# A mixture-of-experts loop: the first 32 blocks without run-time tests, and the next block's rows transposed ahead of the down product

## The reference

```python
# top-1 of 4 groups, top-2 of 8 experts in it; tokens sorted by expert,
# each expert's tokens padded to whole blocks of MOE_BLOCK = 128 rows
rows = jnp.zeros((n_blocks * MOE_BLOCK, D), h.dtype).at[dest].set(h[s_tok])
...
def expert_block(args):
    xb, e = args
    return (jax.nn.silu(xb @ w_gate[e]) * (xb @ w_up[e])) @ w_down[e]

out = lax.map(expert_block, (rows.reshape(n_blocks, MOE_BLOCK, D), blk_expert)).reshape(-1, D)
return jnp.zeros((M, D), h.dtype).at[s_tok].add(out[dest] * s_w[:, None])
```

## Time and profile before

| what | value |
|---|---|
| median of 3 runs | 2845.91 us (2845.04 to 2850.43) |
| the profiled execution's own time | 2846.74 us |
| its span | 2845.0 us |
| mean granted TensorE clock over the span | 0.932 of full speed |
| matmuls of the expert loop, L2385 and L2395 | 450.6 and 225.0 us of PE |
| expert loop | about 2082 us to the end of the span |

### The profile page before, as it was taken

The page is one execution under the profiler, slowest core; times in us unless marked ns, Lnnn a source line. Parts: engine busy times, 40 slices in busy tenths (PEclk is TensorE's granted clock), DMA queues, the critical chain, the costliest instruction groups (busy, mean ns, idle before and its releaser), DMA issues. The chain is left out here.

```text
span 2845.0 us, 32921 instructions
## 1 busy us (share of the span) xinstructions
PE 2515.7 (88%) x12051; PEld 1571.1 (55%) x12051; DVE 784.1 (28%) x1523; ACT 493.2 (17%) x1315; POOL 485.7 (17%) x574
## 2 busy tenths in 40 slices
PE   6999998999779999869816999979779999999996
PEld 4446655888566676647514666634334444444443
DVE  2016442555355655424420000001221111111110
ACT  1101111333024444423200000001100000000000
POOL 1035121343130000100030000011102112211221
PEclk8999999999569999979958999989879999999998
DMA  4010300000220000056255000032258888888894
GB/s 130 30 59 30 127 2 0 1 1 1 63 32 1 1 1 1 13 151 172 68 148 148 30 1 1 0 128 77 107 198 312 313 310 309 318 312 303 310 318 127
DMA packets 186148, 331.25 MB, mean 116 GB/s; under 512 B 32901, under 2 KB 82318, under 8 KB 185822
## 3 DMA queue, kind: packets, MB, share of 16 engines
q1 hardware_dynamic: 160118, 293.08, 30.4%
q0 software_dynamic: 15472, 28.89, 3.6%
q10 hardware_dynamic: 10432, 7.57, 0.9%
HBM read 307.48 MB, written 51.37 MB: 126 GB/s over the span
## 5 line engine op out<-in xcount | busy, mean ns | idle before, releaser
L2385 PE MATMUL psum<-f_W,f_xT 128*128 128x512 f32 x1024 | 450.6, 598 | 17.0 <-DVE f_xT L2431 16.0
L2385 PEld LDWEIGHTS psum<-f_W,f_xT 128*128 128x128 f32 x1024 | 193.0, 191 | 255.8 <-issue 254.6
L1918 PE MATMUL psum<-hT,x_wg 128*128 128x344 f32 x768 | 227.8, 455 | 20.7 <-DMA x_wg<-w_in 20.7
L419 PE MATMUL psum<-w,hT 128*128 128x512 f32 (+3 forms) x576 | 225.5, 552 | 7.1 <-DMA w<-w_in 7.1
L2395 PE MATMUL psum<-f_W,f_aT 128*128 128x512 f32 x512 | 225.0, 592 | 1.2 <-DVE f_aT L2446 1.2
L1918 PEld LDWEIGHTS psum<-hT,x_wg 128*128 128x128 f32 x768 | 146.8, 191 | 97.5 <-DMA x_wg<-w_in 20.8
L419 PEld LDWEIGHTS psum<-w,hT 128*128 128x128 f32 (+1 forms) x576 | 103.6, 182 | 122.7 <-issue 107.6
L419 PE MATMUL psum<-hT,w 128*128 128x344 f32 x576 | 168.9, 454 | 0.0
L2395 PEld LDWEIGHTS psum<-f_W,f_aT 128*128 128x128 f32 x512 | 97.2, 190 | 123.4 <-issue 123.4
L1491 ACT ACTIVATE a_P<-psum,a_nmax 128x512 f32<-128x512 f32 (+4 forms) x256 | 123.0, 494 | 168.5 <-DVE a_nmax L1420 109.2
L2435 DVE TENSOR_TENSOR f_a<-f_sg,psum 128x512 f32<-128x512 f32 x32 | 22.0, 689 | 460.7 <-ACT f_sg L2416 460.7
(11 more groups left out here) (481 smaller groups left out, 3429.6 us busy)
## 6 DMA issues: line engine op xcount, KB each, us to landing
f_W<-w_gate SPq DMA_DIRECT2D x32, 2048.0 KB, 14.2
f_W<-w_up SPq DMA_DIRECT2D x32, 2048.0 KB, 20.3
f_W<-w_down SPq DMA_DIRECT2D x32, 2048.0 KB, 9.5
k_stage<-cache_nsa SPq DMA_DIRECT2D x128, 192.0 KB, 2.6
w<-w_in SPq DMA_DIRECT2D x6, 2048.0 KB, 7.9
x_wg<-w_in SPq DMA_DIRECT2D x8, 1024.0 KB, 13.7
x<-x_prompt SPq DMA_DIRECT2D x8, 512.0 KB, 4.4
o_x<-x_prompt SPq DMA_DIRECT2D x8, 512.0 KB, 4.3
```

Of the source, the lines that this page charges most:

```text
L419: ins = nc.tensor.matmul(PS[i % 4][0:m_rows, 0:n], lhsT, rhs, start=(k == 0), stop=(k == KD - 1))
L1918: ins = nc.tensor.matmul(PS[b + i][:, 0:n], wg[q % 3][:, k, i, c:c + P], hT[:, k, t0:t0 + n], start=(k == 0), stop=(k == KD - 1))
L2385: ins = nc.tensor.matmul(PS[bank][:, :], xT[par][:, k, :], w[par][:, k, :], start=(k == 0), stop=(k == KD - 1))
```

## The change

Three things are changed. First, `each_block` is written in two parts: a loop of 15 rounds and one step more covers the first 32 blocks without any test, and what lies behind block 32 is a second loop of eight rounds with the old tests, the whole of it behind one test n > NE. Second, PE's `transpose_rows` of block b+1 moves from `rest` into `first`, so that it stands behind the gate and up product of b and ahead of the down product of b-1. Third, the copies `copy_rows` on ACT and DVE move along: on ACT behind SiLU, on DVE behind the multiplication by up, both ahead of `copy_out`. POOL's and SP's own functions are the same as before, except that the tests around them are gone.

```diff
-            n = engine.value_load(blocks[0:1, MAXBLK:MAXBLK + 1], min_val=MINBLK, max_val=MAXBLK)
+            n = engine.value_load(blocks[0:1, MAXBLK:MAXBLK + 1], min_val=NE, max_val=MAXBLK)
             first(0, 1, 1, 0)
             rest(0, 1, 1)
-            with engine.Fori(0, MAXBLK // 2) as i:
-                for par, b, number in ((1, 2 * i + 1, i + 1), (0, 2 * i + 2, i + 2)):
-                    with engine.If(b < n):
-                        first(par, number, i + 2, b)
-                    if tail is not nothing:
-                        with engine.If(b < n + 1):
-                            tail(1 - par, i + 1)
-                    if rest is not nothing:
+
+            def step(b, par, i):
+                first(par, i + 1 if par else i + 2, i + 2, b)
+                tail(1 - par, i + 1)
+                rest(par, i + 1 if par else i + 2, i + 2)
+
+            with engine.Fori(0, NE // 2 - 1) as i:
+                step(2 * i + 1, 1, i)
+                step(2 * i + 2, 0, i)
+            step(NE - 1, 1, NE // 2 - 1)
+            with engine.If(n < NE + 1):
+                tail(1, NE // 2)
+            with engine.If(n > NE):
+                with engine.Fori(NE // 2, MAXBLK // 2) as i:
+                    for par, b, number in ((0, 2 * i, i + 1), (1, 2 * i + 1, i + 1)):
                         with engine.If(b < n):
-                            rest(par, number, i + 2)
+                            first(par, number, i + 1 + par, b)
+                        ...
             def load(par, u, u_next, b):
-                if isinstance(b, int):
+                if isinstance(b, int) and b == 0:
                     return
@@ gate_and_up on PE
                 ins.then_inc(gu_done[par], 1)
+                transpose_rows(1 - par, u_next)
@@ transposes on PE
-                transpose_rows(1 - par, u_next)
                 pe.wait_ge(a_done[par], u)
@@ silu on ACT
                 nc.scalar.activation(sg[:, :], PS[2][:, :], ACT.Silu).then_inc(silu_done[par], 1)
+                copy_rows(1 - par, u_next)
-            each_block(act, silu, copy_out, lambda par, u, u_next: copy_rows(1 - par, u_next))
+            each_block(act, silu, copy_out)
@@ copies on DVE
-                copy_rows(1 - par, u_next)
                 dve.wait_ge(atp_done[par], u)
```

More of the change, by code:

```diff
@@ L45 @@
 ROUND = 12582912.0
-MINBLK = 32
 Q0, KC0, VC0, KS0, VS0, KW0, VW0, NG0 = 0, 512, 640, 768, 896, 1024, 1152, 1280
@@ L2294, in each_block @@
             first, tail, rest = first or nothing, tail or nothing, rest or nothing
-            n = engine.value_load(blocks[0:1, MAXBLK:MAXBLK + 1], min_val=MINBLK, max_val=MAXBLK)
+            n = engine.value_load(blocks[0:1, MAXBLK:MAXBLK + 1], min_val=NE, max_val=MAXBLK)
             first(0, 1, 1, 0)
             rest(0, 1, 1)
-            with engine.Fori(0, MAXBLK // 2) as i:
-                for par, b, number in ((1, 2 * i + 1, i + 1), (0, 2 * i + 2, i + 2)):
-                    with engine.If(b < n):
-                        first(par, number, i + 2, b)
-                    if tail is not nothing:
-                        with engine.If(b < n + 1):
-                            tail(1 - par, i + 1)
-                    if rest is not nothing:
-                        with engine.If(b < n):
-                            rest(par, number, i + 2)
+            def step(b, par, i):
[11 more added lines that the diff above has]
+                    for par, b, number in ((0, 2 * i, i + 1), (1, 2 * i + 1, i + 1)):
+                        with engine.If(b < n):
+                            first(par, number, i + 1 + par, b)
+                        if tail is not nothing:
+                            with engine.If(b < n + 1):
+                                tail(1 - par, i + par)
+                        if rest is not nothing:
+                            with engine.If(b < n):
+                                rest(par, number, i + 1 + par)
+                if tail is not nothing:
+                    with engine.If(n > MAXBLK - 1):
+                        tail(1, MAXBLK // 2)
             return n
```

## The result

The changed kernel takes 3075.99 us in the median (3071.39 to 3078.68, 4 runs), the kernel before, in 4 runs, 2847.8 us. The ratio of the runs is 1.080, 95% interval 1.0781 to 1.0818. The forecast was 3065 us, range 2990 to 3112, slower with a chance of 0.94.

A forecast was written before the change was run, and what follows sets the result against it. PE was taken to bound the kernel, 22.70 us a round; the new ring of 20.84 - 0.3 + 0.89 + 6.87 + 2.1 = 30.4 us gave 2846.7 + 231 - 12 = 3065.7, so 3065 us, range 2990 to 3112.

The forecast's parts named there:

- Which input is late: Expert loop: the gathered rows land after PE's moved transposes ask for them, so PE stands for 6.4 us a round.
- D: The end of a down product on PE in the expert loop, from which times in a round are counted.
- PE's wish: When PE's moved transposes ask for the gathered rows: D + 14.45 instead of D + 22.70.
- The landings stay: POOL's scatter and gather in the loop still land after 8.8 and 7.0 us, beside the same weight loads.
- The clock: PE's clock falls to 1.2 GHz in each pause; 4.25 us at half speed after it lose 2.1 us a round.
- The rival without the clock: PE stalls but resumes at 2.4 GHz: a ring of 28.3 us, 3002 us in all; chance 0.17.
- The ring's length: Round of POOL's scatter and gather, their landings, PE's transposes and down: 30.4 us against 22.70.
- the test's: POOL's test between the scatter's landing and the next gather: its removal takes 0.3 us off each round.
- The tests at the end: Empty rounds for blocks 33 to 48 behind the last scatter: one test replaces them, saving 12 us of 14.5.
- What the Trainium skill says of DMA times: GpSimd transfers cost about 2.0 us plus bytes at 436 GB/s: rows at D + 11.4, a round of 22.2 us.
- no stall: Rival: landings shorten, rows arrive by D + 14.45, PE's round is 22.2 us, 2819 us in all; chance 0.05.
- The count: Late rows are those of block 3 through block 32: 30 longer rounds of the expert loop, 231 us.

The follow-up runs named there:

- The run with small weights: Changed kernel with an eighth of the gate and up and of the down weights loaded for each block from 1 on: 2833.3 us.
- the filler: Changed kernel with 7 unused matmuls on PE between the gate and up product and the transposes of the next rows: 3024.2 us, ratio 1.0619.
- the run of the tests alone: Kernel before with the new `each_block`, transposes and copies left in their old places: 2837.0 us, ratio 0.9967.
- that of the order alone: Kernel before with `transpose_rows` and `copy_rows` moved as in the change, all tests kept: 3079.8 us, ratio 1.0818.

## Why the prediction was right, point by point

- **Which input is late** was the step that decided, and it held. The rows' landing at D + 20.84 was expected, in the round above, with D at 2593.06, it is D + 21.04. PE's wish at D + 14.45 was expected, and its last gate and up record ends at 2607.2, D + 14.2. The wait of 6.4 us was 6.6.
- **The landings stay** held: 8.6 and 7.0 us. The run with small weights shows why they are as long as they are.
- **The clock** held in kind and nearly in size. In the round shown it fell 4.3 us into the pause (PE stops at 2607.2, the mean of 0.77 puts the fall at 2611.5) and was back 4.2 us behind the restart (2614.14; the down product in full clock from 2618.4). Over 29 rounds the fall came 2.2 to 4.5 us into the pause, and the return 3.3 to 5.3 us behind the restart, 4.0 in the mean. I had expected 4.25 and a loss of 2.1 us a round; the filler measured 1.98. The rival without the clock, 3002 us, is refuted, since the clock fell in each of these pauses; the run with 7 matmuls, which kept it up, came to 3024. Two readings were off. The trace of the kernel before has eleven pauses of over 5 us that began at 1.00, not seven, and the clock fell in all of them. And the mean clock in the loop is 0.89, not 0.8, because the low stretch is short beside a round of 30.7 us.
- **The ring's length**: 30.4 us expected, 30.71 in the mean of the 28 rounds from 2160 us on, 30.5 over all 30 (the last, beside no weight loads, is 26.3). Without the last, PE restarts at D + 20.78 in the mean, where 20.54 was expected, and transposes and down take 9.94 us, where it was 9.86. The term that was wrong is the test's. It is worth 0.16 us behind the landing and not 0.3, and the new loop takes this back ahead of it: the first scatter's issue is at D + 1.83 in the mean instead of 1.69, with both copies out starting 0.05 to 0.08 us later. This comes with the loop and not with the order, since the run of the tests alone has 1.84 and that of the order alone 1.69. Why the copies start later is open.
- **The tests at the end** were over-sized: 12 us, where 8.1 were measured behind the last landing, and 8.4 with the landing itself, which was 0.4 us shorter. I had left 2.5 us for the program's own end, and it takes 6.0, with 0.5 for the step over the second part. Of the 9 us by which the sum of the differences was low in the profiled executions, this is 3.6, the rounds are 3.5 (234.5 against 231), and 2.1 lie ahead of the first scatter, outside the loop. The page of the Trainium skill ("Advanced Engine Details and Errata", "Control Flow Timing") gave an estimated 3.5 us for 32 tests; no run separates them from the eight returns in the 8.1 us.
- **What the Trainium skill says of DMA times** ("DMA: Bandwidth & Descriptors", "Anatomy of one DMA — SWDGE (gpsimd) path"; an estimated 3.2 us for 512 KB) does not fit even with an eighth of the weights, at 4.3 us for the gather. Its consequence, no stall, would have been nearly right on DMAs with little else to do, as the run with small weights shows (0.5 us of wait a round); beside the weight loads the gather's 7.0 us are more than twice its price. For the scatters the forecast put in too many bytes: they leave out the rows of a block that belong to none of their tokens, and the last block's two carried 0.33 MB between them.
- **The count** of 30 rounds held, with the last one shorter. The sum of the differences in the profiled executions is 234.5 us for the rounds, 3.0 us until the first scatter (0.9 of it the transposes put ahead of the first down product, the rest outside the loop), 1.0 us less for the last down product, and 8.4 us less from the last scatter's issue to the end: 228.1 us, the difference of the spans.

The open points are why the copies out start later in the loop without tests, and what moves the start of the loop by up to 14 us from one program to the next, with the same code ahead of it.

## What to carry to other kernels

An input that causes no wait still has a landing time. Before an instruction is moved forward in an in-order queue, that time must be read for what it waits for; here the cover was 1.9 us and the move took 8.3. A move that saves 0.5 us a round costs 8 us when the engine that feeds it sits behind the moved engine's own output, because the two then form a ring. The cure is on the feeding side: issue the gather ahead of the wait for the scatter, and the moved transposes bring what they promised.

## What the runs showed of the hardware

- A float32 matmul of 128x512 is two instructions of the trace of 0.43 us at 2.4 GHz, 0.86 us in all.
- PE pauses of 6.6 us in a loop of 30.7 us brought the clock down to 1.2 GHz in the pause, and it was back 3.3 to 5.3 us behind it; work of no use in the pause made the kernel 52 us faster.
- An indirect gather of 128 rows of 4 KB landed in 4.3 us, and an accumulating indirect scatter of fewer bytes in 5.1 us, beside an eighth of the weight loads; beside all of them it was 7.0 and 8.6 us. Two scatters issued 1.9 us apart had both landed 10.4 us behind the first issue, a single one after 9.6 us.
- Eight rounds with four failing tests each and the return to the loop's head cost POOL 8.1 us, about 1 us a round. Its last instruction, a drain, took 5.2 us in the kernel before and in the changed one.
